# Reordering the router, the first expert and the last norm in a two-layer trunk step

## The reference

```python
for l in range(2):
    m = silu(c) @ w_ada[l] + b_ada[l]                 # six vectors: shift, scale, gate, twice
    h = rms_norm(x, g_attn[l]) * (1 + scale1) + shift1
    # three head groups read h through one projection: neighbourhood, latent (MLA), windowed attention
    x = x + gate1 * (concat(o_na, o_mla, o_swa) @ w_out[l])
    h = rms_norm(x, g_ffn[l]) * (1 + scale2) + shift2
    scores = sigmoid(h @ w_router)                    # 16 experts in 4 groups
    # the best group by its two best scores + bias, then the top 2 experts in it; weights normalised
    y = sum(weight_e * (silu(h @ w_gate[l, e]) * (h @ w_up[l, e])) @ w_down[l, e])
    x = x + gate2 * y
y = rms_norm(x, g_final)
```

## Time and profile before

| | us |
|---|---|
| three runs | 1252.33, 1253.03 (median), 1255.98 |
| profiled execution, its time | 1255.41 |
| its span, from the first to the last instruction | 1253.4 |
| TensorE busy (share) | 1152.9 (92%) |
| VectorE busy | 772.4 (62%) |
| ScalarE busy | 632.9 (50%) |
| GpSimd busy | 127.8 (10%) |
| mean granted clock of TensorE | 0.947 |

### The profile page before, as it was taken

How to read it: one execution, slowest core, us unless ns; L and a number is a source line. 1 busy time by engine, 2 the same in 40 slices (tenths; PEclk the granted TensorE clock), 3 DMA queues, 4 the chain that set the end, 5 groups by cost and what they waited for, 6 DMA issues and landing times.

```text
span 1253.4 us, 14864 instructions
## 1 busy us (share of the span) xinstructions
PE 1152.9 (92%) x5574; PEld 844.6 (67%) x5574; DVE 772.4 (62%) x1056; ACT 632.9 (50%) x751; POOL 127.8 (10%) x157
## 2 busy tenths in 40 slices
PE   6999998897899999999879998889789999999956
PEld 5576354554788888888666754455578888888846
DVE  1312356427698888888451233742768888988845
ACT  2201455315377777777320035631447777777721
POOL 2241100310100101010010011000000101010000
PEclk9899999999799999999969998999779999999985
DMA  9994478339489999999699140002549999999621
GB/s 330 335 309 169 145 264 280 100 109 377 148 321 372 359 376 366 383 375 367 221 345 240 68 168 16 1 1 81 245 158 352 369 375 378 377 364 369 257 87 75
DMA packets 81257, 314.35 MB, mean 251 GB/s; under 512 B 22766, under 2 KB 27100, under 8 KB 68396
## 3 DMA queue, kind: packets, MB, share of 16 engines
q1 hardware_dynamic: 65548, 279.17, 61.2%
q0 software_dynamic: 13152, 24.96, 6.0%
q10 hardware_dynamic: 2496, 9.44, 2.0%
HBM read 308.11 MB, written 26.38 MB: 267 GB/s over the span
## 4 chain that ended last, share of the span: by engine, by line
PE 84%; DVE 7%; issue 3%; ACT 3%; DMA 2%; SPq 0%; ACTq 0%; POOL 0%; POOLq 0%; DVEq 0%
PE bank L813 17%; PE bank L1072 14%; PE bank L1066 14%; PE bank L1067 14%; PE bank L795 3%; PE bank L941 3%; PE bank L820 3%; PE bank L740 2%; PE bank L1056 2%; PE bank L955 2%; ACT work L1295 2%; PE bank L733 2%; PE bank L973 1%; PE bank L1046 1%; PE bank L874 1%
## 5 line engine op out<-in xcount | busy, mean ns | idle before, releaser
L1791 DVE TENSOR_TENSOR ring_r<-ring,work_r 128x4096 fp32r<-128x4096 f32 x96 | 421.6, 4416 | 0.1
L1352 ACT ACTIVATE work_r<-ring 128x4096 fp32r<-128x4096 f32 x96 | 349.6, 3644 | 138.0 <-PE bank L1067 104.4
L1066 PE MATMUL bank<-work_r 128*128 128x512 f32 x768 | 310.1, 404 | 12.3 <-issue 5.1
L1067 PE MATMUL bank<-work_r 128*128 128x512 f32 x768 | 303.9, 396 | 0.0
L813 PE MATMUL bank<-hT,ring 128*128 128x384 f32 (+1 forms) x640 | 213.7, 493 | 3.3 <-ACT hT L1202 1.9
L1072 PE MATMUL bank<-ring_r,work_r 128*128 128x512 f32 x768 | 195.1, 396 | 0.4 <-DVE ring_r L1791 0.4
L813 PEld LDWEIGHTS bank<-hT,ring 128*128 128x128 f32 (+1 forms) x640 | 121.5, 192 | 88.0 <-issue 11.6
L1066 PEld LDWEIGHTS bank<-work_r 128*128 128x128 f32 x768 | 147.5, 192 | 43.9 <-issue 5.8
L1072 PEld LDWEIGHTS bank<-ring_r,work_r 128*128 128x128 f32 x768 | 144.2, 188 | 34.5 <-DVE ring_r L1791 0.8
L1067 PEld LDWEIGHTS bank<-work_r 128*128 128x128 f32 x768 | 147.1, 192 | 29.6
L1174 ACT ACTIVATE work<-bank 128x384 f32<-128x384 f32 (+6 forms) x79 | 38.0, 494 | 179.7 <-PE bank L813 89.3
(11 more groups left out here) (202 smaller groups left out, 1152.7 us busy)
## 6 DMA issues: line engine op xcount, KB each, us to landing
ring<-in_w_gate SPq DMA_DIRECT2D x32, 2048.0 KB, 11.5
ring<-in_w_up SPq DMA_DIRECT2D x32, 2048.0 KB, 12.3
ring<-in_w_down SPq DMA_DIRECT2D x32, 2048.0 KB, 12.3
ring<-in_w_ada SPq DMA_DIRECT2D x24, 2048.0 KB, 10.0
ring<-in_w_in SPq DMA_DIRECT2D x4, 2048.0 KB, 15.5
work<-yscr ACTq DMA_DIRECT2D x6, 1024.0 KB, 7.1
ring<-in_w_out SPq DMA_DIRECT2D x4, 1280.0 KB, 8.0
ring<-in_w_in SPq DMA_DIRECT2D x12, 256.0 KB, 6.9
```

The lines of the kernel that those rows point to most:

```text
L1066: mm(b[:], x_hi[:, k, :], hi[:, k, half, :], start=(k == 0), stop=False)
L1067: last = mm(b[:], x_lo[:, k, :], hi[:, k, half, :], start=False, stop=False)
L1352: A_(w_hi[:, slot % 2, :], ring[slot][:], ACT.Copy).then_inc(s_hi, 1)
L1791: tt(ring_r[slot][:], ring[slot][:], w_hi[:, slot % 2, :].bitcast(F32), ALU.subtract).then_inc(s_lo, 1)
```

## The change

- **Start.** Only the first 256 columns of the constants are loaded ahead of x; the rest goes behind the four first modulation chunks (one table of 128 columns is dropped). ScalarE issues the small vectors. TensorE sums the squares of four pieces, does A0, sums the last two, does A1, B0, spreads the root, and does the other modulation pieces behind it; the norming of `hT` is then split from its modulation.
- **Router.** The logits are formed from the raw residual: `zT` times `wz` (router weights times gain), block by block, scaled by the root afterwards, plus a product of the router weights with the shift (`wb`, eight small products between `op0` and `op1`). `gains` moves ahead of the output projection. ScalarE modulates all eight blocks of the second norm. The modulation pieces of `ADA_ROUTE` and the turning of rows come behind the turned logits. GpSimd issues the store of the rows.
- **Slots.** One-hots, mask, ranks and table are 16-bit; the weights are in three parts in columns of their own. Only group 0's slots are computed before expert 0; groups 1 to 3 between its two products, the weights by slot behind them. Expert 1's tokens have buffers of their own (`xs1`).
- **End.** No squares' sums and no spread: `zT` is turned, ScalarE squares it from PSUM with an accumulating sum, and VectorE scales the rows from PSUM with the root and `gfin`.

```diff
@@ start: SyncE, TensorE @@
-            sp.dma_start(cst[:], C_dram[:, 0:KEPT_W]).then_inc(s_const, 16)
...
+            sp.dma_start(cst[:, 0:2 * P], C_dram[:, 0:2 * P]).then_inc(s_const, 16)
...
+                    if (l, k) == (0, len(ADA_FIRST)):
+                        sp.dma_start(cst[:, 2 * P:], C_dram[:, 2 * P:KEPT_W]).then_inc(s_const2, 16)
...
+                    for t in range(2):
+                        for h in range(2):
+                            piece_sums(0, t, h)
+                    pe.wait_ge(s_sil, 1)
+                    ada(first[0])
+                    for h in range(2):
+                        piece_sums(0, 2, h)
+                    for j in first[1:3]:
+                        ada(j)
                 spread((l, "n1b"), roots_before(l, 0) + 1)
-                for j in BETWEEN_SPREAD if l else []:
+                for j in BETWEEN_SPREAD if l else first[3:]:
                     ada(j)
@@ router: TensorE @@
+                def router_part(k):
+
+                    read_out(pe, (l, f"op{k}"))
+                    for cond in range(2):
+                        c = sel(cond)
+                        last = mm(bR[32 * (k % 4):32 * (k % 4) + 32, c], wz[:, k, cond, :], zT[:, k, c], start=(k < 4 and cond == 0), stop=(k >= 4),
+                                  skip_group_check=True)
+                    return last
...
+                    if n == 0:
...
+                        for k in range(KT):
+                            last = mm(bN[32 * (k % 4):32 * (k % 4) + 32, 8:10], wb[:, k, :], modT[:, l, 24 + k, :], start=(k < 4),
+                                      stop=(k >= 4), skip_group_check=True)
+                        last.then_inc(s_router, 1)
...
+                for k in range(0, 3):
+                    router_part(k)
...
                 sums_of_added(l)
...
+                for k in range(3, 6):
+                    router_part(k)
                 spread((l, "n2b"), roots_before(l, 1) + 1)
...
+                for k in range(6, KT):
+                    last = router_part(k)
+                last.then_inc(s_router, 1)
...
+                for j in route[0:2]:
+                    ada(j)
+                for h in range(2):
+                    pe.wait_ge(s_ha, (4 + KT) * l + 4 + 4 * (h + 1))
+                    for t in range(NT):
+                        turn4((l, f"hr{t}{h}"), lambda k: hT[:, 4 * h + k, t * P:(t + 1) * P])
+                    for j in route[2:3] if h == 0 else []:
+                        ada(j)
                 for j in route[3:5]:
                     ada(j)
...
                 pe.wait_ge(s_mask, l + 1)
@@ expert 0: TensorE @@
+                    by_slot(0)
+                    if p == 0:
+                        jobs_done()
...
+                    def gate_up(e, slots, between=None):
...
+                        product([bG], *x, slots[0], chunk_no(l, p, e, 0), s_gd)
+                        if between:
+                            between()
+                        product([bU], *x, slots[1], chunk_no(l, p, e, 1), s_gu)
...
                     tokens(0, 0, g0 + 16)
...
+                    def second_tokens_and_slots():
+                        tokens(1, 1, g1 + 16)
+                        for q in range(1, NG):
+                            by_slot(q)
+
+                    gate_up(0, (0, 1), second_tokens_and_slots)
+                    weights_by_slot()
                     turn_a(0)
@@ router: ScalarE @@
+                modulate_second(l, range(2))
+                act.wait_ge(s_logit, l + 1)
+                A_(rw[:, 0, :], rw[:, 0, :], ACT.Exp, scale=-1.0).then_inc(s_rexp, 1)
+                modulate_second(l, range(2, 4))
+                for j in route[0:1]:
                     ada_row(l, j)
...
+                modulate_second(l, range(4, KT))
+                for j in route[1:2]:
+                    ada_row(l, j)
+                for h in range(2):
+                    for t in range(NT):
+                        copy((l, f"hr{t}{h}"), hrow[t][:, 512 * h:512 * (h + 1)], 512)
+                for j in route[2:]:
                     ada_row(l, j)
@@ expert 0: ScalarE @@
                     tokens_upper(0)
+                    tokens_upper(1)
                     upper(1, 0, place(0, 0)[0], 0, place(0, 0)[1])
                     silu(0)
-                    tokens_upper(1)
@@ expert 0: VectorE @@
+                    onehots(0)
+                    slots(0)
+                    if p == 0:
+                        for j in route[5:]:
+                            ada(l, j)
                     rest(0, 0, 0)
-                    slots(NG - 1)
-                    tokens_rest(0)
+                    rest(0, 1, 1)
                     if p == 0:
                         v.wait_ge(s_counted, l + 1)
                         chain(nc.vector.tensor_reduce(cnt[:, 0:1], banks[7][:, 0:NE], AX.X, ALU.max))
                         tc(cnti[:, 0:1], cnt[:, 0:1]).then_inc(s_cnt, 1)
-                    v.wait_ge(s_slot, NG * (n + 1))
-                    rest(0, 1, 1)
+                    tokens_rest(0)
+                    for q in range(1, NG):
+                        onehots(q)
+                    tokens_rest(1)
+                    if p == 0:
+                        weights()
+                    for q in range(1, NG):
+                        slots(q)
+                    gate_weights()
+                    rest(1, 0, place(0, 0)[0])
+                    v.wait_ge(s_gsl, n + 1)
                     activate(0, 0)
-                    tokens_rest(1)
-                    rest(1, 0, place(0, 0)[0])
                     turned_rest(0)
                     rest(1, 1, place(0, 1)[0])
@@ end: VectorE @@
-            rsqrt((DEPTH, 0), D)
-            normalise_last("nfb")
+            v.wait_ge(s_fsq, 2 * NT)
+            chain(nc.vector.tensor_reduce(ns[:, 4, :], fsum, AX.X, ALU.add))
+            chain(ts(ns[:, 0, :], ns[:, 4, :], 1.0 / D, EPS, ALU.mult, ALU.add))
+            chain(newton())
+            v.wait_ge(s_gfin, 16)
             for t in range(NT):
-                b = take(v, f"fo{t}1")
-                evac(f"fo{t}1", tc(xrows[:, t, 512:1024], b[:]))
+                for h in range(2):
+                    half = slice(512 * h, 512 * h + 512)
+                    evac(f"fo{t}{h}", stt(xrows[:, t, half], bank(f"fo{t}{h}")[:], ns[:, 1, t:t + 1], gfin[:, half], ALU.mult, ALU.mult))
```

More of the change, by code:

```diff
@@ L281, in build @@
         WORK = 16384
-        work, work_r = both("work", [P, WORK])
+        work, work_r, work_h = both("work", [P, WORK], halves=True)
         at = [0]
@@ L1029, in _, with jobs_done @@
                 for t in range(NT):
-                    last = mm(banks[7][:, 0:NE], ones, m[:, t, :], start=(t == 0), stop=(t == NT - 1))
+                    last = mm(banks[7][:, 0:NE], onesb[:], m[:, t, :], start=(t == 0), stop=(t == NT - 1))
                 last.then_inc(s_counted, 1)
-                for j in route[5:]:
-                    ada(j)
-                for bk in range(NB):
-                    pe.wait_ge(s_evac[bk], sum(JOB[j][0] == bk for j in LIST[:LIST.index((l, "y00") if l else (1, BETWEEN[0]))]))
+                def jobs_done():
+                    for j in route[5:]:
+                        ada(j)
+                    for bk in range(NB):
+                        pe.wait_ge(s_evac[bk], sum(JOB[j][0] == bk for j in LIST[:LIST.index((l, "y00") if l else (1, BETWEEN[0]))]))
@@ L1529, in normalise @@
                     if k % 2:
[L1530 to L1539 removed]
+                        modulate(l, which, k)
             for l in range(DEPTH):
@@ L1671, in add_squares @@
                     tt(sq_sum, sq_sum, sq_new[n % 2], ALU.add).then_inc(s_sqadd, 1)
+                v.wait_ge(s_mod, ADA_ALL.index((0, 9) if l == 0 else (1, 7)) + 1)
+                chain(gains(l, 1))
+                v.wait_ge(s_bs, 16 * 4)
+                for cond in range(2):
+                    ins = tt(wz[:, :, cond, 0:NE], wr[:], gain[:, 1, :, cond].unsqueeze(2).to_broadcast([P, KT, NE]), ALU.mult)
+                ins.then_inc(s_wz, 1)
                 for n in range(KT):
```

434 lines of the change are left out of this document (249 added, 185 removed).

## The result

The changed kernel takes **1258.61 us** (median of 5 runs, 1257.74 to 1259.94) against 1253.11 (5 runs, 1252.33 to 1257.07) of the kernel before on the same chip: a ratio of **1.0051, 95% interval 1.0029 to 1.0074**. The forecast was 1258.6. The profiled execution took 1258.39 us, its span is 1256.6, 3.2 more than before.

A forecast was written before the change was run, and what follows sets the result against it. TensorE bounds the kernel, busy 100.00 of 100 us in mid-experts. Start -2.4, layer 0 +11.7, layer 1 +4.5 and end -8.2 sum to +5.6 on 1253.0, so 1258.6 us; range 1251 to 1266.

The forecast's parts named there:

- The activation behind expert 1's gate-weight subtraction: Between experts 0's and 1's first products: expert 0's activation waits for a 4.42 us subtraction, part of +8.9 (layer 1 +9.0).
- both subtractions ahead of the tokens': VectorE does expert 0's two weight subtractions before its tokens'; expert 0's first product (gate 0) at 43.5 and 35.1 us.
- one-hots: Router's slot tables on VectorE: 16-bit compares take 0.615 us each, as in 32-bit, not the double rate.
- the cheap end: After the last expert rows: cheaper squares, root and scalings end the kernel 8.2 us sooner (-7 to -9.5).
- the clock's fall in the new gap: Expert 1's first product to its activation (D): 5.6 us gap, then half-speed products, +2.0 layer 0, +0.3 layer 1.
- Rival 2: Experts 2 to 15 absorb the delay before expert 1's first product: +8.9 and +9.0 vanish, 1240.7 us; chance 0.16.
- signs of being wrong: Activation not behind expert 1's gate-weight subtraction, or experts 2 to 15 taking less than 17.9 us each.
- the first gather ... is hidden behind these subtractions: Before expert 0's first product: gather (0.9 us to issue, some 3.6 to land) costs nothing beside VectorE's subtractions.
- rival 4: Rows' store, issued behind GpSimd's queue, and gather take 7 us more; layer 1's gate 0 7 later: 1265.6; chance 0.05.
- Slot products: Between experts 0's and 1's first products: 84 products at 0.06 us each, 5.0 us a layer.
- Products with the shift: Inside the output projection: eight added router products on TensorE cost 1.2 us a layer, between 0.3 and 1.8.
- The start: Up to the input projection: earlier prompt rows and small vectors gain 2.4 us, between 0.7 and 4.6.

The follow-up runs named there:

- e2: Changed kernel with expert 0's activation ahead of the subtraction of expert 1's gate weights in VectorE's list; 1251.8 us, ratio 0.9991 to the kernel before.
- e1: Changed kernel with ScalarE, not GpSimd, issuing the three stores of the rows; 1259.4 us, ratio 1.0047 to the kernel before.
- e5: Changed kernel with SyncE holding its next weight loads until the three stores of the rows have landed; 1256.4 us, ratio 1.0034 to the kernel before.
- e6: Changed kernel with modulation products A0 and A1 back between output projection and spread, B0 between the turned rows; 1250.8 us, ratio 0.9979 to the kernel before.
- e10: e9 with VectorE's first weight subtraction waiting until GpSimd has issued the first gather; 1240.0 us, ratio 0.9870 to the kernel before.
- e4: Changed kernel with SyncE issuing the seven small vector loads ahead of x again; 1257.7 us, ratio 1.0045 to the kernel before.
- e7: Kernel before with only the change's new end; 1241.6 us, ratio 0.9916 to the kernel before.
- e9: Changed kernel with the edits of e6 and e2, and expert 0's token subtraction ahead of the second weight subtraction; 1237.3 us, ratio 0.9861 to the kernel before.
- e12: e11 with one layer 0 load held until the first gather lands, VectorE's second weight subtraction later, more added products; 1232.4 us, ratio 0.9837 to the kernel before.
- e8: Changed kernel with 20 products without use added on TensorE behind the weights by slot; 1254.4 us, ratio 1.0014 to the kernel before.
- e11: e10 with products without use added wherever TensorE idles between the router and expert 1's first product; 1237.2 us, ratio 0.9876 to the kernel before.

## Why the forecast was right, and where it was not

**Right in mechanism.** The activation behind expert 1's gate-weight subtraction (e2), both subtractions ahead of the tokens', one-hots at 0.63 each and no faster (forecast 0.615), the cheap end, the clock's fall in the new gap and its price in sum (D +0.9 and +0.6, forecast +1.6 and -0.1). Rival 2 is out: the delay was not absorbed. One of my signs of being wrong did come, experts 2 to 15 at less than 17.9 us (17.86 against 17.94), but it is worth 1 us a layer, not 9.

**The step that failed** is "the first gather ... is hidden behind these subtractions". I had moved A0 and A1 on TensorE's list and followed their cost there, not the two loads that they release on SyncE's queue. Gate 0 comes 7.5 us later than my reckoning in both layers, which is the size of rival 4 (chance 0.05), in both layers instead of one, and for another cause than the one I gave it: not GpSimd's queue (e1), but the transfers that the stores meet (e5, e6: 7.3 and 5.9 us of layer 0's gate 0, 4.1 of layer 1's in e6), and then, in layer 1, the hold of VectorE's subtraction on GpSimd's gather (3.5, e10).

**Terms mis-sized.** Slot products: 84 at 0.06, measured 36 in 1.05 and 48 in 1.36, 0.029 each; -2.6 a layer, most of the difference between +8.9 and +5.5. Products with the shift: 1.2, measured 0.4. The start: -2.4, measured -0.1. I took the vectors to land earlier because they were issued earlier, and they land later; but e4 shows that early vectors give 0.2 us, so the range of 0.7 to 4.6 was wrong too, since from the turned x on TensorE's own list sets the time (and in e4 the projection's weights). The end: -8.2, measured -11.2 (e7: -11.0); the squares are ready 13.0 us behind the first sum of rows, where I had 15.5, as TensorE's clock was up from 1242.1 to 1249.0, which I had left low.

**Not foreseen and not settled.** The stretch from expert 1 of layer 0 to layer 1's projection is 5.4 us shorter. The experts' period is 17.94 us before and in e7, 17.86 after and in e1 to e9 but e7, 17.96 in e10 to e12, the same in both layers of each; 1.0 us a layer from before to after, its cause not tried, and in layer 0 a longer first period (18.29 against 17.56) leaves 0.2 of it. The other 5.2 us lie behind the last activation and go with the clock: between 600 and 840 us it was at 1.2 GHz for 37.5 us before (and in e7) and for 27.3 after, and from the last activation to layer 1's output projection it took 227.6 and 222.4 us. Over all fourteen kernels these run together, from 23.9 us and 221.7 (e4) to 41.0 and 228.1 (e10). Why the low time differs is open.

The errors above add to +7.5 and +7.4 (gate 0), +2.3 (start), against -6.9 (gate 0 to gate 1), -1.5 (shift), -3.0 (end) and -8.2 (the rest): together 2.4 less in the profile, and nothing in the medians. The profiled execution of the kernel before (1255.41) lay 2.3 us above its median, the one after 0.2 below.

## What to carry to other kernels

When an instruction is moved, follow also the transfers that its end releases: here two products moved by 11 us sent two 2 MB loads into the gap in which 1.5 MB of rows had been stored, and the store took 20 us. A gather issued by GpSimd wants to be ahead of VectorE's long subtractions and of the bulk loads, not among them. Where TensorE idles 5 us ahead of a long run of products, reorder first (e2), and if the gap stays, products without use in it can be worth their place (e8), but look at what the higher clock then releases earlier, and let them end before the operand that TensorE waits for is there (e11, e12: 4.1 and 3.4 us lost).

## What the runs showed of the hardware

- A transfer of small packets that meets bulk loads gets as many packets as they, but few bytes: stores of 0.5 MB in 4 KB packets took 16.5 us (median of three) beside 2 MB loads in 16 KB packets and 3.6 without, from GpSimd's queue and from ScalarE's (15.6) alike; their first packet moved 3.8 us behind the issue instead of 1.1. A gather took 11 us instead of 3.5.
- A gather on GpSimd takes 1.0 to 1.1 us alone and up to 5.2 under one subtraction of VectorE of 4.4 us (128 x 4096, from two operands in SBUF). Under 16-bit one-hots (128 x 512, two operands in SBUF) it took up to 3.1, under 32-bit ones up to 1.35.
- The same experts' loop takes 17.94, 17.86 or 17.96 us an expert, by kernel, to within 0.002 in both layers, with no edit in it.
- 16-bit products with a 128-column load and 3 or 4 columns take 0.029 us each at a granted clock of 1.00.
- The stretches at 1.2 GHz (from 3.4 to 37.6 us long) vary in place between kernels with the same instructions there: the input projection started between 41.1 and 44.0 us in eleven kernels with an equal start. Behind the same wait of 1.92 us ahead of the last expert's down product the clock fell in some traces and not in others.
